# A gated recurrence's 64x64 products on four quarters of the array, its tail interleaved with the next round

## The reference, cut to what matters

```python
def step(state, inp):
    r_t, w_t, k_t, v_t, kk_t, a_t = inp
    sa = jnp.einsum('bhvk,bhk->bhv', state, -kk_t)
    state = (state * w_t[:, :, None, :]
             + sa[..., None] * (kk_t * a_t)[:, :, None, :]
             + v_t[..., None] * k_t[:, :, None, :])
    return state, jnp.einsum('bhvk,bhk->bhv', state, r_t)
...
_, y = lax.scan(step, s0, (tm(r4), tm(w4), tm(k4), tm(v4), tm(kk), tm(a4)))
mean = jnp.mean(y, axis=-1, keepdims=True)
var = jnp.mean(jnp.square(y - mean), axis=-1, keepdims=True)
yn = ((y - mean) * lax.rsqrt(var + RWKV_LN_EPS)).reshape(B, S, RWKV_WIDTH)
...
return ((yn + bonus) * g.astype(f32)).astype(p.dtype)
```

## Time and profile before

| | |
|---|---|
| three runs | 2868.9, 2870.2 (median), 2871.1 us |
| the profiled execution's own time | 2871.36 us |
| its span in the profile | 2869.5 us |
| TensorE busy, whole span | 2745.0 us (96%) |
| stretch of the recurrence, 337.55 to 533.00 us | 195.45 us |
| in it: TensorE, VectorE, ScalarE busy | 170.29, 102.26, 76.37 us |
| in it: mean granted TensorE clock | 0.92 |

### The profile page before, as it was taken

How to read it: one execution, slowest core, us unless ns; L and a number is a source line. 1 busy time by engine, 2 the same in 40 slices (tenths; PEclk the granted TensorE clock), 3 DMA queues, 4 the chain that set the end, 5 groups by cost and what they waited for, 6 DMA issues and landing times.

```text
span 2869.5 us, 48840 instructions
## 1 busy us (share of the span) xinstructions
PE 2745.0 (96%) x17766; PEld 2358.8 (82%) x17766; DVE 2027.0 (71%) x3149; ACT 1399.7 (49%) x2217; POOL 177.8 (6%) x210
## 2 busy tenths in 40 slices
PE   7999988799799999999999999999989999999997
PEld 6878877688588888888886888888868888888886
DVE  5676555577688787888888776668877756665675
ACT  5444443455554444444454455445455545554553
POOL 4600000030100000000020000000100000000002
PEclk9999999899899999999999999999999999999999
DMA  5554200245367778777776874567745555555553
GB/s 192 181 164 163 97 2 2 100 166 188 128 246 281 273 279 292 272 278 279 272 274 222 295 264 164 180 232 276 277 148 184 187 189 181 193 184 188 187 179 137
DMA packets 157857, 573.42 MB, mean 200 GB/s; under 512 B 18000, under 2 KB 18416, under 8 KB 157264
## 3 DMA queue, kind: packets, MB, share of 16 engines
q1 hardware_dynamic: 154368, 562.11, 56.6%
q10 hardware_dynamic: 2208, 7.57, 0.7%
q0 software_dynamic: 1072, 0.89, 0.1%
HBM read 567.64 MB, written 2.10 MB: 199 GB/s over the span
## 4 chain that ended last, share of the span: by engine, by line
PE 83%; DVE 9%; POOL 3%; issue 2%; ACT 2%; DMA 0%; ACTq 0%; DVEq 0%; POOLq 0%
PE ps L2212 44%; PE ps L2213 24%; PE ps L2215 3%; DVE wlo L1896 3%; PE ps L2237 2%; PE ps L2239 2%; PE ps L2238 2%; PE ps L1002 1%; ACT whi L1681 1%; DVE tt L1923 1%; DVE tt L1981 1%; PE ps L1001 1%; PE ps L990 1%; PE ps L1572 0%; POOL tab L285 0%
## 5 line engine op out<-in xcount | busy, mean ns | idle before, releaser
L1896 DVE TENSOR_TENSOR wlo<-raw,whi 128x1024 fp32r<-128x1024 f32 x872 | 1060.9, 1231 | 429.4 <-ACT whi L1681 427.7
L2212 PE MATMUL ps<-xn,whi 128*128 128x512 f32 x3540 | 1259.3, 400 | 11.5 <-issue 5.3
L1681 ACT ACTIVATE whi<-raw 128x1024 fp32r<-128x1024 f32 x872 | 905.0, 1054 | 593.9 <-PE ps L2213 515.0
L2213 PE MATMUL ps<-xn,wlo 128*128 128x256 f32 x3776 | 1052.5, 281 | 0.0
L2212 PE MATMUL ps<-act_in,whi 128*128 128x512 f32 x2444 | 868.5, 400 | 7.7 <-issue 3.4
L2212 PEld LDWEIGHTS ps<-xn,whi 128*128 128x128 f32 x3540 | 667.8, 189 | 177.4 <-issue 11.1
L2213 PE MATMUL ps<-act_in,wlo 128*128 128x256 f32 x2624 | 730.6, 281 | 0.0
L2213 PEld LDWEIGHTS ps<-xn,wlo 128*128 128x128 f32 x3776 | 716.0, 190 | 5.1
L2212 PEld LDWEIGHTS ps<-act_in,whi 128*128 128x128 f32 x2444 | 461.2, 189 | 121.2 <-DVE wlo L1896 5.0
L2213 PEld LDWEIGHTS ps<-act_in,wlo 128*128 128x128 f32 x2624 | 497.6, 190 | 4.0
L1688 ACT ACTIVATE hl<-ps 128x256 f32<-128x256 f32 x416 | 155.3, 375 | 356.9 <-PE ps L2215 356.9
(11 more groups left out here) (329 smaller groups left out, 2226.0 us busy)
## 6 DMA issues: line engine op xcount, KB each, us to landing
raw<-in_stream SPq DMA_DIRECT2D x872, 512.0 KB, 4.2
adaw<-in_ada SPq DMA_DIRECT2D x96, 512.0 KB, 5.9
adaq<-in_ada SPq DMA_DIRECT2D x96, 512.0 KB, 4.8
h<-in_xT SPq DMA_DIRECT2D x4, 512.0 KB, 7.4
memx<-in_memT ACTq DMA_DIRECT2D x1, 2048.0 KB, 9.3
out<-fin SPq DMA_DIRECT2D x4, 512.0 KB, 2.6
lwa<-in_lora ACTq DMA_DIRECT2D x1, 1536.0 KB, 6.9
wst<-in_wsT ACTq DMA_DIRECT2D x1, 1024.0 KB, 8.4
```

The lines of the kernel that those rows point to most:

```text
L1681: act.activation(whi[:, r, :], raw[:, r, :], ACT.Copy).then_inc(hi_done, 1)
L1896: dve.tensor_tensor(wlo[:, r, :], raw[:, r, :], whi[:, r, :].bitcast(F32), ALU.subtract)\
L2212: pe.matmul(ps[:, b, :], whi[:, r, w], x[:, kc, :], start=first, stop=False)
L2213: ins = pe.matmul(ps[:, b, 0:T], wlo[:, r, w], x[:, kc, 0:T], start=False, stop=False)
```

## The change

- `product`, `doubled`, applied values and `applied` move the result of chunk `cc` to the other half of the partitions (`1 - cc`), so that the two kinds of product in `doubled` lie on four quarters instead of two. They go to two banks instead of one (4g and 4g+1). The masked copy of a level becomes two of 128x256 (`x` and `z`); the next `product` waits for `x` alone.
- The chunk products and the products of outputs and states are put in an order that goes round the four quarters. The query and key tile `ar` holds its first half with neighbouring chunks swapped; the instruction that writes it (L731) becomes two of half the size.
- The 8 small products of a lane (L972) become 16: their transposes are made by TensorE too (`first`), and VectorE no longer copies them from `lm`.
- The tail is cut into parts (`mean`, `variance`, `inverse`, `normed`, `low_part`) with counters of their own, and the next round's `chunk_products`, `first` and `applied_v` stand between them. ScalarE fills `xx` (`unit`) before the squares of the tail.
- The turn of lane 0 is moved between the states s1 and s2; the gate is moved behind `product(i, 2)` and waits for the norm's maximum `km`.

```diff
@@ vector: levels, tail
-                if lv < 5:
-                    m = mk[:, lv + 1, :].bitcast(I32).rearrange("p (w c) -> p w c", w=2).unsqueeze(2).to_broadcast([P, 2, 4, CH])
-                    ins = dve.copy_predicated(xx[g][:, :, :, :], m, ps[:, 4 * g + 1, :].rearrange("p (w a c) -> p w a c", w=2, a=4))
...
+                for w in range(2) if lv < 5 else (1,):
+                    cd(i, g, f"z{lv}" if w and lv < 5 else f"x{lv}", dve.copy_predicated(
+                        xx[g][:, w, :, :], level(lv, w).to_broadcast([P, 4, CH]),
+                        (ps[:, 4 * g + 1, 0:T] if w else ps[:, 4 * g, T:2 * T]).rearrange("p (a c) -> p a c", a=4)))
...
-            tail(i)
+            mean(i)
+            if more:
+                masked(i + 1, 0)
+            variance(i)
+            if more:
+                masked(i + 1, 1)
+            inverse(i)
+            if more:
+                first(i + 1)
+            normed(i)
@@ vector, in the loop
             doubled(i, 1)
+            if i:
+                low_part(i - 1)
@@ scalar
             if more:
                 turned_a(act, i + 1)
-            tail(i)
+                unit(i + 1)
+            variance(i)
@@ tensor: chunk products and the small ones
-                for hd in range(2):
-                    for w in range(2):
-                        for c in range(4):
...
+        quads = [(w, b, hd, cc) for w in range(2) for b in range(2) for hd in range(2) for cc in range(2)]
+        def chunk_products(i):
+            for g in lanes:
+                q = 2 * (i % 2) + g
+                PA.wait(pe, g, i, "tc")
...
+                for w, b, hd, cc in quads:
...
+        def first(i):
+            for g in lanes:
+                q = 2 * (i % 2) + g
+                if i:
+                    YD.wait(pe, g, i - 1, "ve")
...
+        def applied_v(i):
+            for g in lanes:
+                CD.wait(pe, g, i, "l1")
@@ tensor: doubled
+                if lv > 1:
+                    CD.wait(pe, g, i, f"z{lv - 1}")
                 for u in range(4):
                     for cc in range(2):
-                        k = rows(cc)
+                        k, f = rows(cc), rows(1 - cc)
                         if lv < 5:
-                            mm(ps[k, 4 * g + 1, u * CH:(u + 1) * CH], xx[g][k, 1, u, :], pp[g][k, u, :], start=True, stop=True)
-                        ins = mm(ps[k, 4 * g + 1, T + u * CH:T + (u + 1) * CH], pp[g][k, u, :], xx[g][k, 1, u, :],
-                                 start=True, stop=True)
+                            mm(ps[k, 4 * g, T + u * CH:T + (u + 1) * CH], xx[g][f, 1, u, :], pp[g][f, u, :], start=True, stop=True)
+                        ins = mm(ps[f, 4 * g + 1, u * CH:(u + 1) * CH], pp[g][f, u, :], xx[g][f, 1, u, :], start=True, stop=True)
@@ tensor: states and the loop
             for c in (1, 2):
+                if c == 2 and i < 3:
+                    turn_t(pe, i + 1, (0,))
...
-            start(i)
+            applied_v(i)
+            if i:
+                inverse(i - 1)
             product(i, 1)
...
-            if more:
-                gate_t(pe, i + 1)
             product(i, 2)
+            if more:
+                gate_t(pe, i + 1)
...
             if more:
-                turn_t(pe, i + 1)
+                turn_t(pe, i + 1, (1,))
...
-            tail(i)
+            mean(i)
+            if more:
+                chunk_products(i + 1)
+            variance(i)
+            if more:
+                first(i + 1)
```

More of the change, by code:

```diff
@@ L371, in scalar, with unit @@
         act.dma_start(lwa1[:, :, :, :], A["lora"][2:8].rearrange("n p b c -> p n b c")).then_inc(lw_in, 16)
-        def start(i):
+        def unit(i):
             for g in lanes:
@@ L750, in vector, with masked @@
         level = lambda lv, w: mk[:, lv + 1, w * CH:(w + 1) * CH].bitcast(I32).unsqueeze(1)
-        def start(i):
-            for g in lanes:
-                CT.wait(dve, g, i, "ll")
-                for hd in range(2):
-                    cd(i, g, f"l{hd}", dve.tensor_tensor(lm[g][:, hd, :, :], tri(ps[:, 4 * g + hd, :]), m_tri, ALU.mult))
+        def masked(i, g):
+            CT.wait(dve, g, i, "ll")
+            for hd in range(2):
+                cd(i, g, f"l{hd}", dve.tensor_tensor(lm[g][:, hd, :, :], tri(ps[:, 4 * g + 2 + hd, :]), m_tri, ALU.mult))
+        def first(i):
             for g in lanes:
@@ L798, in state, with yd_, mean @@
                         nn[g][:, c, :], ALU.mult, ALU.add))
-        def tail(i):
+        def yd_(i, g, name, ins, chain=False):
+            YD.done(ins, g, name)
+            if chain:
+                YD.wait(dve, g, i, name)
+        def mean(i):
             for g in lanes:
@@ L924, in bonus_t, with turn_t @@
             PT.done(pe.matmul(bank(i, g, "bs")[:, 0:T], blk[:, 0, :], bp[i][g][:, :], start=True, stop=True), g, "bs")
-    def turn_t(pe, i):
-        for g in lanes:
+    def turn_t(pe, i, which=lanes):
+        for g in which:
             q = 2 * (i % 2) + g
@@ L1026, in applied @@
                 CT.done(ins, g, "ry")
             for g in lanes:
[L1028 to L1035 removed]
+                for step, c, hd in [(0, 1, 0), (0, 2, 0), (0, 1, 1), (0, 2, 1)] + [
+                        (step, c, hd) for cs_ in ((0, 1), (2,)) for step in (1, 2) for hd in range(2) for c in cs_]:
+                    o, b, f = rows(c % 2), c // 2, rows(hd)
+                    bank, n_at = 4 * g + (0 if c == 1 else 3), (1, 1, 2)[c] * CH
+                    if step == 0:
+                        mm(ps[f, bank, 0:CH], pa[g][o, hd, b, 0:CH], tm[i][g][o, 0, b, f], start=True, stop=True)
+                    elif step == 1:
@@ L1056, in applied, with mean, variance @@
                 CT.done(ins, g, "yy")
-        def tail(i):
+        def mean(i):
             for g in lanes:
-                CD.wait(pe, g, i, "yd")
-                CT.done(mm(ps[:, 4 * g, 0:T], blk[:, 1, :], y1[g][:, :], start=True, stop=True), g, "mu")
+                YD.wait(pe, g, i, "yd")
+                YT.done(mm(ps[:, 4 * g, 0:T], blk[:, 1, :], y1[g][:, :], start=True, stop=True), g, "mu")
+        def variance(i):
             for g in lanes:
-                CA.wait(pe, g, i, "yq")
+                YA.wait(pe, g, i, "yq")
                 for b in range(2):
@@ L1091, in turned_p @@
             HT.done(ins, 0, f"pt{k}")
+        chunk_products(0)
+        first(0)
         for i in range(4):
             more = i < 3
-            start(i)
+            applied_v(i)
+            if i:
+                inverse(i - 1)
             product(i, 1)
```

193 lines of the change are left out of this document (101 added, 92 removed).

## The result

The changed kernel takes 2845.9 us (median of 4 runs, 2842.4 to 2849.6), the kernel before beside it 2870.7 (2868.9 to 2871.7): ratio 0.991, 95% interval 0.9899 to 0.9922. The forecast was 2842.5 with 2833 to 2857.

The account below looks back on a forecast made before the run. TensorE, using half of itself, was taken to bound the touched 195.45 us stretch. Gains of 2.2, 3.0, 8.8, 14.6 and 1.6 make 30.2 us, less 2.5 for clock 27.7: 2843.7 profiled, median 2842.5, range 2833 to 2857.

Parts of the forecast that it names:

- start to P1: Stage's start, 7.68 us: lane 0 is masked while lane 1 still waits, P1 after 5.5, gain 2.2 us.
- levels, rounds 0 to 2: D1 to D5, with preparation between the levels: gains 3.2, 2.8 and 2.8, together 8.8 us.
- levels, round 3: Four levels at period 2.40 instead of 3.43 give 4.1 us; round 2's normalization holds them 1.05: gain 3.0.
- borders at full clock: D5 to the next P1, 24.91 us: P1 at 20.05, gain 4.85, three times: 14.6 us.
- clock: In the touched stretch: 10 us more at 1.2 GHz, at the lower price, cost 2.5 us.
- the rival with the floor: Four-quarter records come no closer than L972's 0.018 us: 3 us less gain, 2845.5; no chance of its own given.
- I count this step as nothing: Border, D5 to the states: outputs and states gain about 0.2 us, as VectorE still writes the next round's keys.
- outside the stretch nothing moves: Sign to look for: before and behind the touched stretch of 195.45 us no time changes.
- No fourfold rate: Rival, 8%: dense products gain nothing from four quarters; half copies, border overlap and ends leave 15 us, 2855.
- The border holds: Rival, 10%: VectorE's ordered waits each 1 us longer, a border gives 1.9 instead of 4.85: 9 us less, 2851.5.
- The clock falls: Rival, 9%: waits in every level put the remaining 165 us at 1.2 GHz, 32 to 63 us more, profile 2873 to 2904.
- half case: Half of the fall to 1.2 GHz in the whole stretch, 5%: 2852 to 2864 us.

Follow-up runs that it names:

- the slow order alone: The kernel with mended waits, with outputs and states in the order on two quarters in rounds 0 to 2: 2838.2 us, ratio 0.9875.
- mended waits: Changed kernel with round 1's lora products later, keys' scaling ahead of the low parts, round 2's normalization split by lane: 2840.5 us, ratio 0.9891.
- halves alone: The kernel before with only the level copies cut in halves, products still on two quarters: 2871.3 us, ratio 0.9991.
- three fillers: The kernel with mended waits, plus three throwaway TensorE products per round ahead of the bonus products in rounds 0 to 2: 2837.8 us, ratio 0.9877.
- one kind after the other: Changed kernel with all doubled products of one kind issued before those of the other in each level: 2840.5 us, ratio 0.9901.
- outputs on two quarters: Changed kernel with the products of outputs and states in the old order on two quarters: 2840.4 us, ratio 0.9884.

## Why the prediction was right, and what was off in it

| term, us | forecast | measured in the profile after |
|---|---|---|
| start to P1 | 2.2 | 0.85 (7.68 to 6.83) |
| P1 to D1, round 0 | 0 | -3.5 (3.84 to 7.38, clock 0.77) |
| levels, rounds 0 to 2 | 8.8 | 8.6 (from 19.60, at full clock, to 16.88 twice and 16.44) |
| levels, round 3 | 3.0 | 3.3 (13.71 to 10.37) |
| borders at full clock | 14.6 | 16.7 (24.91 to 19.35, three times) |
| the last end | 1.6 | 1.5 (19.39 to 17.90) |
| clock | -2.5 | +1.9 in the stage (the rest of its 29.4) |
| outside the stage | 0 | -6.2 |

The mechanism was right in the levels and at the border. That the total came within 3.4 us is partly luck: the terms missed by 0.1 to 6 us with both signs, and the misses partly cancel.

- **Four quarters.** I took 0.015 us per record from one place with a mean of 0.018. The 64 doubled records of both lanes (442.53 to 443.48) start within 0.95 us: 0.015 each. The Trainium skill ("TensorE: Matmul & The Clock Gate", the section on why a gap is 56 and not 53.3 ns) says that starts never come closer than about 25 ns; this trace does not agree for products on four quarters, and the rival with the floor is out.
- **Levels.** The period was forecast as a chain through three engines, 2.40; it is 2.42 to 2.43. The parts of round 1 were forecast as 4.9, 3.6, 2.7 and 5.7 and are 4.91, 3.55, 2.68 and 5.74. The normalization costs round 3 0.64, not 1.05.
- **Border.** The forecast chain is what happened, 0.7 shorter. The failed step is "I count this step as nothing", of outputs and states: on four quarters they are worth 0.52, though TensorE then stands 1.46 us for VectorE. So the mean is at 12.3 after D5 and not at the forecast 12.85, and all behind it comes 0.5 sooner: chunk products 13.3 (13.75), variance 15.2 (15.7). The forecast had the squares behind `unit` hold the variance; TensorE is busy with the chunk products just as long, and when these took 0.6 longer, the variance came 0.6 later. The spread is at 18.3 (19.0), P1 at 19.35 (20.05).
- **Start.** The failed step is "lane 0 is masked while lane 1 still waits". VectorE does the input projection's additions until lane 1 can go as well (all four masks follow each other, 2.48 us), so only the shorter products count.
- **P1 to D1 of round 0**, taken as unchanged: the low-rank weights landed 4.1 us after P1, TensorE waited 1.7 us for them and then did the products at 1.2 GHz. I had not priced this load against the shorter way from the stage's start to it. In five other profiles, where it landed 1.5 us sooner after its issue, it cost 0.5.
- **Clock.** I put 10 us more at 1.2 GHz into the stage. There it is less: twice 0.07 of 166, some 23, against 31. The terms above add up to 27.5, and 1.9 more came from such stretches that the kernel before had elsewhere, which makes the 29.4 of the stage. The failed step is "outside the stretch nothing moves": 6.2 us were lost there. Before the stage the clock goes with most of it: 340.04 at 0.98, 337.55 at 0.99, 336.52 at 1.00 in the profile of the slow order alone; the change does not reach there, so these 2.5 us need not be its own. Behind the stage the seven profiles of the changed kernel and of those built on it without mended waits have 2338.5 to 2340.2, the five with mended waits 2336.6 to 2338.0, the kernel before and the one with halves alone 2336.5 and 2336.8. More time at 1.2 GHz is not enough to explain it: the changed kernel and the one with three fillers have some 76 us of it there, and 2340.2 and 2337.1. Why is open. The profiled gain was so 23.2 for a forecast 27.7, and the median 3.4 above the forecast.
- **Rivals.** No fourfold rate: out. The border holds: out, the border gave more. The clock falls: out as a fall of the whole stage, but in its smaller form it moves these kernels by as much as most edits do. Its half case was summed too low: half of 32 to 63 us on top of 2841.2 gives 2857 to 2873, not 2852 to 2864; nothing else hangs on it. The first rival also counted 15 levels in one place and 16 in another, and the half copies alone proved worth 2.8 us, not 4.5. In two borders of one profile, 22.93 at 0.78 and 19.35 at 1.00, 10 us at 1.2 GHz cost 3.6: 0.35 per us, inside the forecast's 0.24 to 0.47.

## What to carry to other kernels

Before a dense group is moved to all four quarters, write down the chain through the other engines: it, not TensorE's rate, sets the period afterwards. A copy cut in halves is worth what its first half is early (0.24 to 0.29 us per level in round 3) only where nothing else stands in the chain; in rounds 1 and 2 of the changed kernel it was worth 0.03 to 0.05 in four levels. Moving work into the gap of a serial tail gave more (4 us per border) than the faster products there (1.1 shown, 1.5 at most). When a stage gets shorter, price each load and each wait at its beginning again, and judge edits of a few us by stretches at equal clock: here the totals moved by more, from the clock alone, than most single edits.

## What the runs showed that I had not expected

- Products on other quarters than their predecessors start before these have ended even when the order is one kind or one head behind the other: 64 records in 1.35 us, against 0.95 interleaved, and 0.037 against 0.027 us per record for the chunk products. An order is no clean switch between two and four quarters.
- Kernels that were slower or equal in every stretch at equal clock (one kind after the other, outputs on two quarters) had medians of 2840.5 and 2840.4, below the changed kernel's 2845.9 and 2847.9, with a granted clock in the stage of 1.00 and 0.96 against 0.93. The intervals of their ratios overlap or touch, so this is a warning about small differences and no ranking.
- A stage full of waits of TensorE can run wholly at 2.4 GHz: 158.10 us at clock 1.00 with 17.7 us of them in it (busy 140.36).
